# Every 512-column product names its columns from the last to the first: a two-block transformer on one core

## The chip, the core and the metric

The kernel runs on one core of a Trainium2 chip. The metric is device time in microseconds (us), the median of the timed runs. A core has a matrix engine (TensorE, PE in the profile; its weight loads are the row PEld), a vector engine (VectorE, DVE), a scalar engine (ScalarE, ACT), GpSimd (POOL) and a queue engine that issues transfers (SyncE, SP). They share the on-chip memory SBUF, and TensorE writes its sums to PSUM: 128 partitions with 8 banks of 512 32-bit numbers each.

## What is computed

The reference runs two blocks over 512 tokens of width 1024, all in 32-bit floats, cut here to what matters:

```
# first block
h = rmsnorm(x);  z = h @ w_in                        # latents, heads, two gates
qa = rmsnorm(q_lat) @ w_qb;  kva = rmsnorm(c_kv) @ w_kvb
oa = attention(qa, ka, va);  ob = attention(qb, kb, vb)      # 8 heads each
x += (sigmoid(gate_a) * (oa @ w_oa) + sigmoid(gate_b) * (ob @ w_ob)) @ w_o
x += (relu(rmsnorm(x) @ w_up) ** 2) @ w_down
x += sigmoid(rmsnorm(x) @ w_ple_gate) * (p @ w_ple)
x = rmsnorm(x)
# second block, layer 0: gated delta rule; layer 1: attention with a forget gate
for layer in 0, 1:
    x += rmsnorm(mixer[layer](rmsnorm(x)))           # w_in, w_out; w_kv, w_q, w_o
    x += rmsnorm(swiglu(rmsnorm(x)))                 # 1024 -> 2 * 2816 -> 1024
```

Nearly all arithmetic is in the products with weight matrices.

## The kernel before

**How a product is made.** Activations are held with features on the partitions and the 512 tokens along a partition, so a tile of 128 features is 128x512. To keep 32-bit accuracy each operand is split into a high part, rounded to the matrix engine's one-pass 32-bit type (`fp32r`), and a low part with what the rounding left. A product of a weight tile and an activation tile is then three matmuls into the same PSUM bank: high weight by high activation, high by low, low by high. The helper `product` (L437 to L443) issues these three. The helper `product_by_parts` (L446 to L458) does the same for the first weight chunk of a stage, but in the order in which the activation's parts become ready: the two matmuls on the high part (L452, L453) for two banks, then the one on the low part (L456) for both.

**What is stationary and what moves.** One operand of a matmul is loaded into the array, 128 columns of it (the weight load, PEld). The other, the moving tile, streams through in 512 columns; column j of it gives column j of the sum in the bank. In most stages the weights are stationary and the tokens move; where the result is wanted with tokens on the partitions (the gates and values of the second block, the last down product) the activations are stationary and 512 columns of the weights move. Both helpers are given the bank and the moving tile as 512 neighbouring elements per partition.

**What sets the order.** Weights come in chunks of 128x2048 that SP loads into two buffers in turn. ScalarE rounds a chunk to its high part (L223), VectorE subtracts to get the low part (L250), and TensorE waits for that and works the chunk off. The order on each engine is written out by hand, stage by stage; semaphores tie the engines together, and a bank is read by ScalarE or VectorE only once the last matmul of its sum has counted up `products`. Attention scores (L876), transposes, sums of squares and the small products of the delta rule call the matrix engine directly and not through the two helpers.

Of the kernel before, what the change touches and what calls it, by code (L numbers as in the profile page):

```python
# [4 lines left out]
P = 128  # L5
# [3 lines left out]
DT = D // P  # L9
# [382 lines left out]
def build_program(nc, w, plan, constants, tables, out):  # L392
# [11 lines left out]
    def place(name, at, shape, dtype=mybir.dt.float32):  # L404

        under = int(at * 256)
        if under == 0:
            with nc.sbuf_tensor(name, shape, dtype) as tensor:
                return tensor
        with nc.sbuf_tensor(name + "_under", [P, under], mybir.dt.float32), nc.sbuf_tensor(name, shape, dtype) as tensor:  # L410
            return tensor
# [5 lines left out]
    with ctx:  # L417
# [7 lines left out]
        psum = enter(nc.psum_tensor("psum", [P, 8, T], f32))  # L425
# [7 lines left out]
        def gain(name, tile=0):  # L433
            at = GAIN_AT[name] + tile
            return gains[:, at:at + 1]

        def product(bank, w_parts, a_parts, first, last):  # L437

            (wh, wl), (ah, al) = w_parts, a_parts  # L440
            nc.tensor.matmul(bank, wh, ah, start=first, stop=False)  # L441
            nc.tensor.matmul(bank, wh, al, start=False, stop=False)  # L442
            return nc.tensor.matmul(bank, wl, ah, start=False, stop=last)  # L443

        def product_by_parts(pe, k, banks, w_parts, x_parts, high_done, low_done):  # L446

            (wh, wl), (xh, xl) = w_parts, x_parts
            columns = [(bank, slice(m * P, (m + 1) * P)) for m, bank in enumerate(banks)]
            pe.wait_ge(high_done, k + 1)  # L450
            for bank, sl in columns:
                nc.tensor.matmul(psum[:, bank, :], wh[:, k, sl], xh, start=k == 0, stop=False)  # L452
                nc.tensor.matmul(psum[:, bank, :], wl[:, k, sl], xh, start=False, stop=False)  # L453
            pe.wait_ge(low_done, k + 1)
            for bank, sl in columns:
                last = nc.tensor.matmul(psum[:, bank, :], wh[:, k, sl], xl, start=False, stop=k == DT - 1)  # L456
                if k == DT - 1:
                    last.then_inc(weights.products, 1)  # L458

# [7 lines left out]
        def front(gates, split, q_a, k_a, v_a, qk_b, v_b):  # L467
# [25 lines left out]
            with stage("front", 152) as s:  # L493
# [23 lines left out]
                with nc.Block() as block:  # L517
# [15 lines left out]
                    def _(pe):  # L533
# [52 lines left out]
                        for k in range(DT):  # L586
                            product_by_parts(pe, k, (0, 1), (high, low), (split[:, 0, k, :], split[:, 1, k, :]),
                                             entry.high_done, entry.low_done)
# [7 lines left out]
                        for k in range(DT):  # L596
                            last = product(psum[:, 3, :], (high[:, k, at], low[:, k, at]),
                                           (split[:, 0, k, :], split[:, 1, k, :]), k == 0, k == DT - 1)
# [17 lines left out]
                        for n in range(Q_TILES):  # L616
                            bank = free(first_q + n)
                            for k in range(2):
                                last = product(psum[:, bank, :], [y[:, k, n * P:(n + 1) * P] for y in parts],
                                               (q_split[:, 0, k, :], q_split[:, 1, k, :]), k == 0, k == 1)  # L620
                            last.then_inc(weights.products, 1)
# [9 lines left out]
                        for j in range(TT):  # L631
                            if j >= 2:
                                pe.wait_ge(k_read, 2 * j - 2)
                            product(psum[:, 4 + j % 2, :], [y[:, 0, j * P:(j + 1) * P] for y in parts],
                                    latent, True, True).then_inc(weights.products, 1)
                            product(psum[:, free(first_v + j), :], [y[:, j * P:(j + 1) * P] for y in latent],
                                    [y[:, 0, HEADS * NOPE:] for y in parts], True, True).then_inc(weights.products, 1)
# [433 lines left out]
        class NextEntry:  # L1071
# [39 lines left out]
            def first_chunks(self, pe, start, banks):  # L1111

                lag = 1 if start + 1 in weights.apart else 4
                for i in range(DT + lag):
                    for c, k in ((0, i), (1, i - lag)):
                        if not 0 <= k < DT or 2 * c >= len(banks):
                            continue
                        if k == 0:
                            pe.wait_ge(weights.low_ready, start + c + 1)
                        high, low = weights.parts(Chunk(start + c), DT)  # L1120
                        if c == 0:
                            product_by_parts(pe, k, banks[0:2], (high, low), (self.split[:, 0, k, :], self.split[:, 1, k, :]),
                                             self.high_done, self.low_done)
                            continue
                        for m in range(2):
                            sl = slice(m * P, (m + 1) * P)
                            last = product(psum[:, banks[2 * c + m], :], (high[:, k, sl], low[:, k, sl]),
                                           (self.split[:, 0, k, :], self.split[:, 1, k, :]), k == 0, k == DT - 1)
                            if k == DT - 1:
                                last.then_inc(weights.products, 1)  # L1130
# [102 lines left out]
        class MixerOut:  # L1233
# [9 lines left out]
            def tensor(self, pe):  # L1243
                start, merged = self.start, self.merge.merged
                pe.wait_ge(self.merge.product_read, 12)
                pe.wait_ge(weights.low_ready, start + 1)
                high, low = weights.parts(Chunk(start), DT)
                for k in range(DT):
                    product_by_parts(pe, k, (0, 1), (high, low), (merged[:, 0, k, :], merged[:, 1, k, :]),
                                     self.merge.high_ready, self.merge.low_done)  # L1250
                for t in range(2, DT):
                    if t % 2 == 0:
                        pe.wait_ge(weights.low_ready, start + t // 2 + 1)
                    if t >= 4:
                        pe.wait_ge(self.added, t - 3)
                    whole_tile(start + t // 2, t % 2, t % 4, merged)
# [1974 lines left out]
        merged, part = place("merged", 64, [P, 2, DT, T], f32r), place("part", 96, [P, 2, 4, T])  # L3231
# [9 lines left out]
        columns, scratch = place("gdn_kept_columns", 120, [P, 8, TT * GH]), place("gdn_scratch", 121, [P, 6, T])  # L3241
# [86 lines left out]
        for name in ("ffn0", "fox_in", "ffn1"):  # L3328
            first = weights.start[name]
# [110 lines left out]
```

## Time and profile before

| | |
|---|---|
| median of 3 runs | 2165.18 us (2163.93 to 2165.28) |
| the profiled execution | 2162.32 us |
| its span, first to last instruction | 2160.5 us |
| TensorE busy | 2095.5 us (97%), 10710 matmuls |
| VectorE busy | 1146.3 us (53%) |
| ScalarE busy | 816.6 us (38%) |
| mean granted TensorE clock | 0.987 of full speed |

The profile is of one execution. Busy time is the union of an engine's instructions; the end of a matmul is modelled, and neighbouring matmuls overlap in it, so the pace of a stream of matmuls is read from their start times and not from their durations. An instruction's row names its operands' shape and type; the step between elements is not in it.

### The profile page before, as it was taken

How to read it: one execution, taken by the hardware profiler on the slowest of the kernel's cores; microseconds unless marked ns; L12 is line 12 of the kernel's file. 1: busy time of each engine (PE TensorE's matmuls, PEld its weight loads, DVE VectorE, ACT ScalarE, POOL GpSimd, SP SyncE). 2: the span in 40 equal slices, each digit the busy share in tenths (PEclk: the TensorE clock that was granted, in tenths of full speed). 3: DMA queues.
4: the chain of work that ended last, by engine and by line, in shares of the span. 5: the costliest groups of instructions: out<-in, count | busy, mean ns of one | idle time of the engine just before them, and what ended most of it. 6: DMA issues, size and time to landing. Idle time of an engine off the chain costs nothing. (4 is left out here: it accounts for less than half of the span.)

```text
span 2160.5 us, 26090 instructions
## 1 busy us (share of the span) xinstructions
PE 2095.5 (97%) x10710; PEld 1697.5 (79%) x10710; DVE 1146.3 (53%) x1706; ACT 816.6 (38%) x1169; POOL 38.4 (2%) x34
## 2 busy tenths in 40 slices
PE   8999999999999999999999999999999899999998
PEld 6876678888888887787878888887786577888886
DVE  5674765542542579888846444324634736444423
ACT  4324753331232465542534222213325734322212
POOL 0120000000000000000100000000000000000000
PEclk9999999999999999999999999999999999999999
DMA  4220012223223222233122222222240031222221
GB/s 177 86 83 35 2 59 99 94 95 109 85 96 103 91 81 100 108 117 97 40 98 74 95 95 94 95 96 95 98 173 23 1 118 59 98 98 98 98 98 68
DMA packets 43111, 190.68 MB, mean 88 GB/s; under 512 B 15520, under 2 KB 16224, under 8 KB 22384
## 3 DMA queue, kind: packets, MB, share of 16 engines
q1 hardware_dynamic: 40656, 184.78, 25.0%
q10 hardware_dynamic: 2336, 4.23, 0.6%
q8 instruction: 85, 1.39, 0.3%
q14 instruction: 34, 0.28, 0.0%
HBM read 185.25 MB, written 3.74 MB: 87 GB/s over the span
## 5 line engine op out<-in xcount | busy, mean ns | idle before, releaser
L250 DVE TENSOR_TENSOR weights_low<-weights_raw,weights_high 128x2048 fp32r<-128x2048 f32 (+1 forms) x161 | 365.8, 2272 | 565.4 <-ACT weights_high L223 565.3
L441 PE MATMUL psum<-split,weights_high 128*128 128x512 f32 x1448 | 568.3, 392 | 8.3 <-PEq L146 4.2
L442 PE MATMUL psum<-split,weights_high 128*128 128x512 f32 x1448 | 564.6, 390 | 0.0
L443 PE MATMUL psum<-split,weights_low 128*128 128x512 f32 x1448 | 564.6, 390 | 0.0
L223 ACT CAST weights_high<-weights_raw 128x2048 fp32r<-128x2048 f32 (+1 forms) x161 | 304.0, 1888 | 545.3 <-PE psum L443 504.7
L441 PEld LDWEIGHTS psum<-split,weights_high 128*128 128x128 f32 x1448 | 272.2, 188 | 70.3 <-issue 8.4
L443 PEld LDWEIGHTS psum<-split,weights_low 128*128 128x128 f32 x1448 | 272.0, 188 | 57.4
L442 PEld LDWEIGHTS psum<-split,weights_high 128*128 128x128 f32 x1448 | 272.0, 188 | 56.0
L443 PE MATMUL psum<-hidden_high,weights_low 128*128 128x512 f32 x256 | 99.6, 389 | 0.0
L441 PE MATMUL psum<-hidden_high,weights_high 128*128 128x512 f32 x256 | 99.6, 389 | 0.0
L442 PE MATMUL psum<-hidden_low,weights_high 128*128 128x512 f32 x256 | 99.6, 389 | 0.0
L2042 ACT ACTIVATE ring<-ring 128x512 f32<-128x512 f32 x44 | 27.8, 632 | 117.4 <-DVE ring L2072 117.4
L441 PE MATMUL psum<-hidden,weights_high 128*128 128x512 f32 x176 | 68.5, 389 | 0.0
L442 PE MATMUL psum<-hidden,weights_high 128*128 128x512 f32 x176 | 68.5, 389 | 0.0
L442 PE MATMUL psum<-weights_low,hidden 128*128 128x512 f32 x176 | 68.5, 389 | 0.0
L441 PE MATMUL psum<-weights_high,hidden 128*128 128x512 f32 x176 | 68.5, 389 | 0.0
L443 PE MATMUL psum<-hidden,weights_low 128*128 128x512 f32 x176 | 68.5, 389 | 0.0
L443 PE MATMUL psum<-weights_high,hidden 128*128 128x512 f32 x176 | 68.5, 389 | 0.0
L452 PE MATMUL psum<-split,weights_high 128*128 128x512 f32 x112 | 48.0, 428 | 17.3 <-DVE weights_low L250 10.2
L2530 DVE SCALAR_TENSOR_TENSOR gdn_spare<-psum,conv,gdn_spare 128x511 f32<-128x511 f32 (+2 forms) x72 | 53.8, 747 | 11.0 <-ACT gdn_spare L2363 9.3
L938 DVE TENSOR_REDUCE attn_small<-psum 128x1 f32<-128x512 f32 x64 | 42.5, 688 | 30.6 <-PE psum L876 30.6
L442 PEld LDWEIGHTS psum<-hidden_low,weights_high 128*128 128x128 f32 x256 | 48.0, 188 | 10.1
(485 smaller groups left out, 3081.4 us busy)
## 6 DMA issues: line engine op xcount, KB each, us to landing
weights_raw<-in_weights SPq DMA_DIRECT2D x161, 1024.0 KB, 4.9
minus_c<-minus_c_rows ACTq DMA_DIRECT2D x16, 256.0 KB, 7.3
x_stream<-in_x SPq DMA_DIRECT2D x4, 512.0 KB, 7.1
gdn_in_grown<-gdn_rows SPq DMA_DIRECT2D x4, 512.0 KB, 4.7
chain_grown<-gdn_rows SPq DMA_DIRECT2D x4, 512.0 KB, 3.7
out<-end_results SPq DMA_DIRECT2D x8, 256.0 KB, 2.1
table<-rope_tables SPq DMA_DIRECT2D x1, 1024.0 KB, 12.0
weights_raw<-in_weights SPq DMA_DIRECT2D x1, 768.0 KB, 4.2
```

The source lines that it names most:

```text
L223: self.nc.scalar.copy(self.high_of(chunk.first)[:, 0:width], self.raw[:, chunk.slot, 0:width]).then_inc(self.high_ready, 1)
L250: self.nc.vector.tensor_tensor(out=self.low_of(n)[:, 0:width], in0=self.raw[:, n % 2, 0:width], in1=self.high_of(n)[:, 0:width].bitcast(se ...
L441: nc.tensor.matmul(bank, wh, ah, start=first, stop=False)
L442: nc.tensor.matmul(bank, wh, al, start=False, stop=False)
L443: return nc.tensor.matmul(bank, wl, ah, start=False, stop=last)
L452: nc.tensor.matmul(psum[:, bank, :], wh[:, k, sl], xh, start=k == 0, stop=False)
L938: nc.vector.tensor_reduce(small[:, 0, u:u + 1], psum[:, u % 4, 0:n], AX.X, ALU.max, negate=True).then_inc(max_ready, 1)
L2042: nc.scalar.activation(self.tanh[:, f % 2, :], self.gate[:, f % 2, :], ACT.Tanh, scale=0.5).then_inc(self.tanh_ready, 1)
L2530: nc.vector.scalar_tensor_tensor(out=mixed[:, o % 2, back:T], in0=psum[:, bank_of(o), 0:T - back], scalar=conv[:, at:at + 1], in1=mixed[:, ...
```

## The change

A small helper gives a view of a tile with its columns in descending order (a step of -1, beginning at the last element). Both product helpers take this view of the moving tile and of the PSUM bank. Column j of the moving tile still gives column j of the bank; only the order in which the columns are named in the instruction is turned round. The stationary tile, the matmuls that don't go through the two helpers, and everything on the other engines stay as they were. The instructions of each of the five engines, with their waits, are the same in number and order as before.

```
+        def from_the_end(tile):
+            return tile[:, ::-1]
+
         def product(bank, w_parts, a_parts, first, last):
-            (wh, wl), (ah, al) = w_parts, a_parts
-            nc.tensor.matmul(bank, wh, ah, start=first, stop=False)
-            nc.tensor.matmul(bank, wh, al, start=False, stop=False)
-            return nc.tensor.matmul(bank, wl, ah, start=False, stop=last)
+            (wh, wl), (ah, al) = w_parts, (from_the_end(part) for part in a_parts)
+            out = from_the_end(bank)
+            nc.tensor.matmul(out, wh, ah, start=first, stop=False)
+            nc.tensor.matmul(out, wh, al, start=False, stop=False)
+            return nc.tensor.matmul(out, wl, ah, start=False, stop=last)

         def product_by_parts(pe, k, banks, w_parts, x_parts, high_done, low_done):
-            (wh, wl), (xh, xl) = w_parts, x_parts
-            columns = [(bank, slice(m * P, (m + 1) * P)) for m, bank in enumerate(banks)]
+            (wh, wl), (xh, xl) = w_parts, (from_the_end(part) for part in x_parts)
+            columns = [(from_the_end(psum[:, bank, :]), slice(m * P, (m + 1) * P)) for m, bank in enumerate(banks)]
             pe.wait_ge(high_done, k + 1)
             for bank, sl in columns:
-                nc.tensor.matmul(psum[:, bank, :], wh[:, k, sl], xh, start=k == 0, stop=False)
-                nc.tensor.matmul(psum[:, bank, :], wl[:, k, sl], xh, start=False, stop=False)
+                nc.tensor.matmul(bank, wh[:, k, sl], xh, start=k == 0, stop=False)
+                nc.tensor.matmul(bank, wl[:, k, sl], xh, start=False, stop=False)
             pe.wait_ge(low_done, k + 1)
             for bank, sl in columns:
-                last = nc.tensor.matmul(psum[:, bank, :], wh[:, k, sl], xl, start=False, stop=k == DT - 1)
+                last = nc.tensor.matmul(bank, wh[:, k, sl], xl, start=False, stop=k == DT - 1)
```

## Rows read from the trace of the kernel before

**Rows 1.** The page: busy time (share of span) and instructions; granted clock by slice.

```profile
PE 2095.5 (97%) x10710; PEld 1697.5 (79%) x10710; DVE 1146.3 (53%) x1706; ACT 816.6 (38%) x1169; POOL 38.4 (2%) x34
...
PEclk9999999999999999999999999999999999999999
```

**Rows 2.** Who waited for whom, TensorE: us in total, times, longest.

```profile
PE psum L452 <- DVE weights_low L250: 10.2, 1, 10.2
PE psum L889 <- DVE ring L959: 8.1, 8, 1.7
PE psum L452 <- ACT split L1087: 7.1, 3, 2.4
```

**Rows 3.** Busy time and count, whole span, of L441, L442, L443, L452, L453, L456.

```profile
0.00:2161.00 2161.00, 960.69 (x2452) 460.19 (x2452) 0.99 0.26 88
...
0.00:2161.00 2161.00, 955.95 (x2452) 460.20 (x2452) 0.99 0.26 88
...
0.00:2161.00 2161.00, 955.96 (x2452) 460.14 (x2452) 0.99 0.26 88
...
0.00:2161.00 2161.00, 60.52 (x144) 29.03 (x144) 0.99 0.26 88
...
0.00:2161.00 2161.00, 59.41 (x144) 29.21 (x144) 0.99 0.26 88
...
0.00:2161.00 2161.00, 47.09 (x144) 28.22 (x144) 0.99 0.26 88
```

**Rows 4.** Timeline of TensorE in the first block's down product: start us, us, instruction.

```profile
500.09 0.39 PE L441 MATMUL psum<-hidden_high,weights_high 128*128 128x512 f32 x1
500.31 0.39 PE L442 MATMUL psum<-hidden_low,weights_high 128*128 128x512 f32 x1
500.54 0.39 PE L443 MATMUL psum<-hidden_high,weights_low 128*128 128x512 f32 x1
...
501.45 0.39 PE L441 MATMUL psum<-hidden_high,weights_high 128*128 128x512 f32 x1
```

**Rows 5.** Stretches: from:to, us, each engine's busy us (x instructions), then granted clock.

```profile
500.00:580.00 80.00, 80.00 (x355) 66.24 (x354) 29.38 (x28) 17.29 (x12) 0.00 (x0) 1.00 0.27 92
...
1498.20:1508.40 10.20, 7.13 (x18) 5.22 (x19) 8.61 (x15) 5.75 (x10) 0.00 (x0) 0.50 0.00 1
```

**Rows 6.** Timeline of TensorE at the start of the forget block's products.

```profile
1505.21 0.63 PE L452 MATMUL psum<-split,weights_high 128*128 128x512 f32 x1
1505.64 0.63 PE L453 MATMUL psum<-split,weights_low 128*128 128x512 f32 x1
1506.07 0.63 PE L452 MATMUL psum<-split,weights_high 128*128 128x512 f32 x1
1506.49 0.63 PE L453 MATMUL psum<-split,weights_low 128*128 128x512 f32 x1
1506.92 1.05 PE L456 MATMUL psum<-split,weights_high 128*128 128x512 f32 x2
```

**Rows 7.** Attention scores: a stretch, then line L876's durations (ns) and timeline.

```profile
188.00:242.00 54.00, 53.01 (x359) 33.40 (x360) 35.00 (x75) 35.76 (x90) 0.00 (x0) 1.00 0.00 1
...
L876 PE MATMUL psum<-k_a,q_a x64: 591/592/697, 189.0 to 242.1; 96*128 96x512 f32 x64
...
195.09 1.88 PE L876 MATMUL psum<-k_a,q_a 96*128 96x512 f32 x4
```

**Rows 8.** Timeline of ScalarE and VectorE, 500 to 510 us, with idle time before.

```profile
499.66 1.91 ACT L223 CAST weights_high<-weights_raw 128x2048 fp32r<-128x2048 f32 x1 [8.97 <-PE psum L443]
...
501.60 2.29 DVE L250 TENSOR_TENSOR weights_low<-weights_raw,weights_high 128x2048 fp32r<-128x2048 f32 x1 [8.59 <-ACT weights_high L223]
```

**Rows 9.** Timeline of the end: TensorE's last matmul and VectorE's last work.

```profile
2150.94 0.39 PE L443 MATMUL psum<-weights_high,hidden 128*128 128x512 f32 x1
...
2156.12 1.20 DVE L1882 TENSOR_TENSOR end_results<-end_results,turned_x 128x512 f32<-128x512 f32 x1
```

## The prediction, made before the changed kernel had run

> **What bounds the kernel now.** I read the page's table of busy time first. TensorE is busy 2095.5 us of a span of 2160.5 us, VectorE about half of it, ScalarE a third, and the granted clock stands at nine tenths or more in every slice [rows 1]. Then the table of waits, for TensorE alone: the longest entry is one wait of 10.2 us at the very start, and the next come to 8.1 and 7.1 us [rows 2]. So TensorE is the bound nearly everywhere, and what happens to its pace goes into the time one for one.
>
> Next, how much of that pace the change touches. The six lines of the two product helpers, counted over the whole span, give 2452 matmuls on each of three lines and 144 on each of the other three [rows 3]: 3 x 2452 + 3 x 144 = 7788 matmuls, all with 512 moving columns. Their durations cannot be added up, since 390 ns records overlap. The pace is in the start times: from 500.09 to 501.45 us six starts pass [rows 4], 1.36 us / 6 = 0.227 us each. The stretch from 500 to 580 us says the same over a longer run: 80 us fully busy with 354 weight loads, one for each matmul, 80 / 354 = 0.226 us at a granted clock of 1.00 [rows 5]. I take 0.2265 us. 7788 x 0.2265 = 1764 us, or 82% of the span, is spent in matmuls that the change rewrites.
>
> What that pace is made of matters below. At the full clock (the upper level, 2.4 GHz) 512 columns at one per cycle take 512 / 2.4 = 213.3 ns, so 13.2 ns of each product are something fixed. In a stretch where the granted clock was 0.50 (the lower level, 1.2 GHz) [rows 5], with TensorE at work for only 7.13 of 10.20 us, the same products start at 1505.21, 1505.64, 1506.07, 1506.49 and 1506.92 us [rows 6]: 1.71 / 4 = 0.4275 us, which is 512 / 1.2 = 426.7 ns and next to nothing fixed.
>
> **The change, part by part.** It removes no instruction, adds none and moves none. Each engine has the same instructions in the same order with the same waits, so there is no queue in which something new stands, no transfer that starts at another moment for its own sake, and no wait that takes the place of another. Every one of the 7788 matmuls has the same number of columns. The stationary tile, and with it the weight load, is named as before. What is left is one question asked 7788 times: does TensorE take 512 columns in descending order as fast as in ascending order, when it reads them from SBUF and when it adds them into the bank?
>
> No row of the trace answers it. The records hold no step, and in the program before, every moving tile of the 7788 runs upwards. So I bound the price of one product from both sides.
>
> Below: the stream itself cannot go faster than one column per cycle at the upper clock level, which is 213.3 ns. If the descending order did away with the whole fixed part, a product would gain 13.2 ns: 7788 x 13.2 ns = 103 us.
>
> Above: the nearest rows in which 512 columns take longer on this engine both give about 0.43 us. One is the half clock just read. The other is at a granted clock of 1.00: the scores of the first attention, products of the ordinary 32-bit type, in which four matmuls of 512 columns take 1.88 us with a last one of 592 ns [rows 7], (1.88 - 0.592) / 3 = 0.429 us from start to start, half the pace of the one-pass type at the same clock. If descending columns were served one by one where ascending ones are served in pairs, this is the pace that I expect. The difference is 0.429 - 0.2265 = 0.2025 us per product, times 7788 = 1577 us. A few tens of the products run at the half clock already, which takes some 10 us off.
>
> Which value I take: zero. The nearest row is the product itself, with the same number of elements in the same places: 512 neighbours in SBUF, 512 neighbours in one bank. The sum is 2162.3 us (the profiled execution: its span of 2160.5 us and 1.8 us around it) + 7788 x 0 = 2162.3 us. The median of the runs shown is 2165.2 us, 2.9 us or 0.13% above this execution, and as nothing is added to either I name the median: 2165.2 us.
>
> Here a rule speaks against the change. The Trainium skill, "PSUM — Partial Sum Buffer", section "Specifications (TRN2)", gives PSUM lines of 8 bytes and says that any non-contiguous access pattern slows matmuls significantly; it names no price. By it, if a step of -1 counts as non-contiguous, the sum would be somewhere above 2165 us. "Advanced Engine Details and Errata" of the Trainium skill, section "Memory Cachelines", words it so that every two consecutive elements should be contiguous for best throughput; by that wording columns 511 and 510, which share a line, are as good as 0 and 1, and the sum stays. No run here has shown a stepped product, so the trace does not yet decide between the two.
>
> **What lies beside it.** If the products stay at their pace, nothing else can move, because everything else is cued by them. ScalarE's rounding of a chunk takes 1.91 us after 8.97 us of idling for TensorE, and VectorE's subtraction 2.29 us after 8.59 us of idling for ScalarE [rows 8]. With that much idle time they stay off the path, and all the more if TensorE becomes slower. After the last matmul, which starts at 2150.94 us, VectorE works until 2156.12 + 1.20 = 2157.3 us [rows 9], 3.2 us before the span ends; this tail reads complete banks and does not care in which order their columns were filled.
>
> **The rivals.**
>
> First, pairs that are lost. TensorE at the upper clock level reads or adds two neighbours in one access only if the second lies above the first; descending, each column needs an access of its own. For it: the ordinary 32-bit type shows that this engine does run at 0.429 us per 512 columns when it has to [rows 7], and with 97% busy nothing would hide it. Against it: that pace belongs to another type, and no row ties it to addresses. It decides for the whole kernel as soon as one side, reading or adding, has the limit. Price: 2162 + 1577 - 10 = about 3730 us. The first of the two wordings of the Trainium skill above, on "PSUM — Partial Sum Buffer", points the same way.
>
> Second, a start-up cost per product. Each matmul begins at the far end of its tile and of its bank, and if the first fetch then covers less than it does now, some nanoseconds are added that the stream cannot make good. For it: the fixed 13.2 ns at the full clock [rows 4, 5] show that there is something at the seam between two products. Against it: at the half clock nothing is left of it [rows 6], and the 512 elements begin and end on the same borders in both directions. Price: from 1 ns (7.8 us, 2173 us) to as much again as now, 13.2 ns, 2165 + 103 = 2268 us. It becomes measurable from 0.56 ns per product.
>
> Third, the other sign: the fixed part shrinks, for instance if the seam is a matter of the last columns of one sum being added while the first of the next arrive. Against it: both directions jump from one end of the bank to the other between two products. Price: 2165 - 103 = 2062 us if all of it goes.
>
> That the change does not do what it says, because the order is turned back on the way to the chip, would give 2165 us as well and belongs to the main case.
>
> **How the numbers follow.** A measurement of this kernel can tell about 0.2%, 4.3 us, from no change; per product that is 0.56 ns. Chances: no change 0.77, lost pairs 0.08, a start-up cost 0.10, a gain 0.05. So faster by over 0.2% has 0.05, within 0.2% 0.77, slower by over 0.2% 0.18. The predicted time is that of the likeliest case, 2165.2 us. The range reaches into the neighbouring cases: down to 2150 us, a gain of 2 ns per product (7788 x 2 ns = 16 us), and up to 2205 us, a cost of 5 ns per product (39 us). With 0.77 inside, about 0.06 of the start-up case and 0.02 of the gain, it holds about 0.85. Left out are lost pairs, whose 3730 us would make a range of which nine tenths is empty, and the far ends of the other two.
>
> **What would show it right or wrong.** Right: in the down product around 500 us the starts are still 0.226 to 0.227 us apart, the stretch of 80 us still holds about 354 weight loads, and TensorE's busy time is within a few us of 2095.5. Lost pairs: starts 0.43 us apart at a granted clock of 1.00, while the attention scores keep their own pace, and longer waits of ScalarE's rounding for TensorE. Start-up cost: starts a few nanoseconds further apart, evenly in all stages, and no other row changed. A gain: starts nearer to 0.213 us. I am wrong in kind if the starts in [rows 4] are the same after the change and the time is not; then something other than the stream reads the order of the columns.

## The result: 2% slower, and the profile after

The changed kernel takes 2207.27 us (2206.16 to 2209.87), the kernel before 2165.14 us beside it: a ratio of 1.0198, 95% interval 1.018 to 1.0215. No change had been forecast, with a range up to 2205 us. The profiled execution's span is 2205.1 us, against 2160.5 us.

TensorE is as much the bound as before. The page's row of busy time after, which answers to [rows 1], shows 46.7 us more on PE and next to nothing on the others:

```profile
PE 2142.2 (97%) x10710; PEld 1698.2 (77%) x10710; DVE 1146.6 (52%) x1706; ACT 814.9 (37%) x1169; POOL 38.5 (2%) x34
```

The counts of the product lines (now L445, L446, L447 and L456, L457, L460) are those of [rows 3]. The first and the fourth of these rows after, in the same columns:

```profile
0.00:2206.00 2206.00, 979.30 (x2452) 460.40 (x2452) 0.99 0.25 86
...
0.00:2206.00 2206.00, 60.76 (x144) 28.77 (x144) 0.99 0.25 86
```

So the time went into the pace of the same matmuls. The timeline of TensorE after, in the same down product as [rows 4] (start us, us, instruction):

```profile
500.20 0.40 PE L446 MATMUL psum<-hidden_low,weights_high 128*128 128x512 f32 x1
500.43 0.40 PE L447 MATMUL psum<-hidden_high,weights_low 128*128 128x512 f32 x1
500.67 0.40 PE L445 MATMUL psum<-hidden_high,weights_high 128*128 128x512 f32 x1
...
501.60 0.40 PE L446 MATMUL psum<-hidden_low,weights_high 128*128 128x512 f32 x1
```

Six starts in 1.40 us are 0.2333 us each, where six took 1.36 us before. The stretches, columns as in [rows 5], say it for 80 us at a granted clock of 1.00, and give a stretch at the half clock:

```profile
500.00:580.00 80.00, 80.00 (x345) 64.46 (x343) 24.85 (x21) 14.74 (x8) 0.00 (x0) 1.00 0.27 92
1531.90:1538.80 6.90, 5.99 (x14) 4.47 (x15) 6.87 (x12) 4.97 (x8) 0.00 (x0) 0.51 0.00 0
```

343 weight loads stand where 354 stood. At the half clock nothing has changed; the timeline there answers to [rows 6]:

```profile
1535.64 0.63 PE L456 MATMUL psum<-split,weights_high 128*128 128x512 f32 x1
1536.07 0.63 PE L457 MATMUL psum<-split,weights_low 128*128 128x512 f32 x1
1536.50 0.63 PE L456 MATMUL psum<-split,weights_high 128*128 128x512 f32 x1
1536.92 0.63 PE L457 MATMUL psum<-split,weights_low 128*128 128x512 f32 x1
1537.35 1.05 PE L460 MATMUL psum<-split,weights_high 128*128 128x512 f32 x2
```

(1537.35 - 1535.64) / 4 = 0.4275 us, as before. The attention scores, which keep their order, have the median duration of [rows 7], 592 ns:

```profile
L880 PE MATMUL psum<-k_a,q_a x64: 591/592/1061, 192.7 to 247.5; 96*128 96x512 f32 x64
```

The other engines only wait longer: VectorE's 137 waits for a rounded chunk come to 589.2 us, 565.3 before. And the sum closes to within 3 us. Over all pairs of neighbouring product starts at the full clock that are less than 260 ns apart, the mean is 226.91 ns before and 233.35 ns after: 6.44 ns x 7788 = 50.2 us. The span grew by only 44.6 us, because this execution spent less time at the half clock: with mean granted clocks of 0.987 and 0.991 the clock cost 0.013 x 2160.5 = 28 us before and 0.009 x 2205.1 = 20 us after, which leaves 42 us of the 50.2.

### The profile page after: what moved, and what is told of

Read it like the earlier page. It is cut to its first block and busy times, and to the rows that moved or that the text cites. A ratio compares the mean times of both kernels' runs of the same rounds, so it can differ in the third digit from the quotient of the medians.

```text
span 2205.1 us, 26090 instructions
## 1 busy us (share of the span) xinstructions
PE 2142.2 (97%) x10710; PEld 1698.2 (77%) x10710; DVE 1146.6 (52%) x1706; ACT 814.9 (37%) x1169; POOL 38.5 (2%) x34
## 5 line engine op out<-in xcount | busy, mean ns | idle before, releaser
L250 DVE TENSOR_TENSOR weights_low<-weights_raw,weights_high 128x2048 fp32r<-128x2048 f32 (+1 forms) x161 | 365.4, 2270 | 589.3 <-ACT weights_high L223 589.2
L445 PE MATMUL psum<-split,weights_high 128*128 128x512 f32 x1448 | 578.7, 400 | 8.0 <-PEq L146 4.5
L446 PE MATMUL psum<-split,weights_high 128*128 128x512 f32 x1448 | 575.5, 397 | 0.0
L447 PE MATMUL psum<-split,weights_low 128*128 128x512 f32 x1448 | 575.4, 397 | 0.0
L445 PEld LDWEIGHTS psum<-split,weights_high 128*128 128x128 f32 x1448 | 272.0, 188 | 77.0 <-issue 7.2
L447 PEld LDWEIGHTS psum<-split,weights_low 128*128 128x128 f32 x1448 | 271.9, 188 | 66.0
L446 PEld LDWEIGHTS psum<-split,weights_high 128*128 128x128 f32 x1448 | 272.0, 188 | 64.0
L445 PE MATMUL psum<-hidden_high,weights_high 128*128 128x512 f32 x256 | 101.7, 397 | 0.0
L446 PE MATMUL psum<-hidden_low,weights_high 128*128 128x512 f32 x256 | 101.7, 397 | 0.0
L447 PE MATMUL psum<-hidden_high,weights_low 128*128 128x512 f32 x256 | 101.7, 397 | 0.0
L445 PE MATMUL psum<-hidden,weights_high 128*128 128x512 f32 x176 | 69.9, 397 | 0.0
L447 PE MATMUL psum<-hidden,weights_low 128*128 128x512 f32 x176 | 69.9, 397 | 0.0
L445 PE MATMUL psum<-weights_high,hidden 128*128 128x512 f32 x176 | 69.9, 397 | 0.0
L446 PE MATMUL psum<-hidden,weights_high 128*128 128x512 f32 x176 | 69.9, 397 | 0.0
L446 PE MATMUL psum<-weights_low,hidden 128*128 128x512 f32 x176 | 69.9, 397 | 0.0
L447 PE MATMUL psum<-weights_high,hidden 128*128 128x512 f32 x176 | 69.9, 397 | 0.0
L456 PE MATMUL psum<-split,weights_high 128*128 128x512 f32 x112 | 48.0, 428 | 17.0 <-DVE weights_low L250 9.9
L447 PEld LDWEIGHTS psum<-hidden_high,weights_low 128*128 128x128 f32 x256 | 48.1, 188 | 11.7
```

The source lines that it names most:

```text
L250: self.nc.vector.tensor_tensor(out=self.low_of(n)[:, 0:width], in0=self.raw[:, n % 2, 0:width], in1=self.high_of(n)[:, 0:width].bitcast(se ...
L445: nc.tensor.matmul(out, wh, ah, start=first, stop=False)
L446: nc.tensor.matmul(out, wh, al, start=False, stop=False)
L447: return nc.tensor.matmul(out, wl, ah, start=False, stop=last)
L456: nc.tensor.matmul(bank, wh[:, k, sl], xh, start=k == 0, stop=False)
```

## The experiments

The mean start distances below are taken as just described, between neighbouring matmuls of the same kind. "Up" is from the first column to the last, "down" the reverse.

**Reading or adding.** e1 turns only the moving tile round, e2 only the bank (shortened; `product_by_parts` likewise):

```
# e1: product                        # e2: product
-            out = from_the_end(bank) -  (ah, al) = ..., (from_the_end(part) for part in a_parts)
+            out = bank               +  (ah, al) = ..., a_parts
```

> Only the moving tile is named from the last column to the first; the bank is named upwards as before (the sums land with their columns turned round, so the output is not the reference's). In the changed kernel the products start 233.4 ns apart at the full clock, before 226.7 ns. Theory A (the reading of the moving tile costs the 6.7 ns): starts 233 to 234 ns apart, time about 2207 us, ratio to before 1.02. Rival B (the adding into the bank costs it): starts 226 to 227 ns apart, about 2165 us, ratio 1.00. Rival C (each side costs a part): starts near 230 ns, about 2186 us. In all of them 427 ns at the half clock.

> Only the bank is named from the last column to the first; the moving tile is named upwards as before (the sums land with their columns turned round, so the output is not the reference's). Theory A (the reading costs): starts 226 to 227 ns apart, about 2165 us, ratio 1.00. Rival B (the adding costs): starts 233 to 234 ns apart, about 2207 us, ratio 1.02. Rival C (each a part): near 230 ns, about 2186 us.

e1 took 2206.94 us, ratio 1.0203 (1.0185 to 1.0222); e2 2163.16 us, ratio 1.0003 (0.9991 to 1.0014). Timeline of e1:

```profile
519.81 0.40 PE L445 MATMUL psum<-hidden_high,weights_high 128*128 128x512 f32 x1
520.05 0.40 PE L446 MATMUL psum<-hidden_low,weights_high 128*128 128x512 f32 x1
520.28 0.40 PE L447 MATMUL psum<-hidden_high,weights_low 128*128 128x512 f32 x1
520.51 0.40 PE L445 MATMUL psum<-hidden_high,weights_high 128*128 128x512 f32 x1
```

and of e2:

```profile
519.87 0.39 PE L445 MATMUL psum<-hidden_high,weights_high 128*128 128x512 f32 x1
520.10 0.39 PE L446 MATMUL psum<-hidden_low,weights_high 128*128 128x512 f32 x1
520.32 0.39 PE L447 MATMUL psum<-hidden_high,weights_low 128*128 128x512 f32 x1
520.55 0.39 PE L445 MATMUL psum<-hidden_high,weights_high 128*128 128x512 f32 x1
```

Three starts take 0.70 us in e1 and 0.68 us in e2. The whole cost comes with the order in which the moving tile is read; adding into the bank downwards costs nothing that these runs can tell (their interval ends at 1.0014).

**Per matmul or per column.** e3 splits each matmul into two of 256 columns, e4 does so with each half downwards (shortened):

```
+            for n, half in enumerate((slice(0, 256), slice(256, 512))):
+                done = nc.tensor.matmul(from_the_end(bank[:, half]), w, from_the_end(a[:, half]), ...)   # e4
```

> Every product matmul of 512 columns is made as two of 256 columns, both upwards; the base line for the next run. If the fixed 13.3 ns at the full clock belong to each matmul: 106.7 + 13.3 = 120 ns from start to start, about 240 ns for a pair and about 2165 + 7788 x 0.0133 = 2269 us. If they belong to each 512 columns: about 113 ns, 2165 us, unless the weight load of each holds it up.

> The same two matmuls of 256 columns, each with its moving tile and its part of the bank named from the last column to the first. Theory S (a start-up cost of each matmul): starts 6.7 ns further apart than with the halves upwards, so the time is about 15576 x 6.7 ns = 104 us above that run. Rival D (a cost that grows with the columns, 6.7 ns for 512): 3.3 ns further apart, about 52 us above it.

One run each: 2257.68 us up and 2234.14 us down; neighbours under 140 ns apart start 120.0 and 118.3 ns apart on the mean. For e3 that is its first case, a fixed part that belongs to each matmul. Of e4's two theories both failed, in sign. The stretch from 500 to 580 us of e3, then of e4:

```profile
500.00:580.00 80.00, 80.00 (x669) 80.00 (x668) 16.45 (x8) 14.49 (x8) 0.00 (x0) 1.00 0.27 93
```

```profile
500.00:580.00 80.00, 80.00 (x678) 80.00 (x678) 18.28 (x12) 13.40 (x7) 0.00 (x0) 1.00 0.29 95
```

More matmuls pass downwards than upwards in the same time, so at 256 columns a downward matmul has no dearer start than an upward one. The pair has a limit: there are twice as many weight loads, and they are busy for all of the 80 us (66.24 us in [rows 5]), so that the loads may set part of this pace was not tested.

**Lengths and turns.** e5 varies the middle matmul of each product, e7 turns every second one (shortened):

```
+  down(bank, wh, ah); nc.tensor.matmul(bank[:, 0:448][:, ::-1], w, a[:, 0:448][:, ::-1], ...); down(bank, wl, ah)   # e5, one of 17
+  step = -1 if turns[0] % 2 else 1;  nc.tensor.matmul(bank[:, ::step], w, a[:, ::step], ...)                       # e7
```

> The middle matmul of each product (high weights by low activations) is given other lengths and directions, 20 products at a time, each on its own line; the other two go over 512 columns, all down where the middle one is down, all up where it is up, and mixed in two of the cases. Columns that the middle matmul leaves out are missing from the sums. From 226.7 ns (512 up), 120.05 ns (256 up), 233.35 ns (512 down) and 118.4 ns (256 down) two lines follow. Theory D2 (going down the columns themselves are slower, 0.449 ns each against 0.417, and the fixed part is smaller, 3.5 ns against 13.4): down 448, 384, 320, 256 columns take 204.6, 175.9, 147.2, 118.4 ns; up 200.0, 173.4, 146.7, 120.0 ns; the two cross near 300 columns. Rival S2 (the same 0.417 ns per column both ways, and a seam between two matmuls that depends on where the one stops and the next begins): going down from a place to column 0, N/2.4 + 20 ns whatever N is: 206.7, 180.0, 153.3, 126.7 ns; and a matmul up among ones down, or down among ones up, has yet another seam, so those two cases differ from 226.7 and 233.35 ns. By D2 alone a down matmul among ones up keeps its 0.449 ns per column, 229.9 ns plus a fixed part.

> Every second product matmul is named downwards, the others upwards, moving tile and bank alike. Theory D2 (slower columns going down, a fixed part that belongs to each direction): starts by turns 226.7 and 233.35 ns apart, mean 230, time about 2165 + 3894 x 6.65 ns = 2191 us, ratio 1.012. Rival S2 (the seam is set by where the one stops and the next begins): an up matmul stops at column 511 where the next, down, begins, and that one stops at column 0 where the next begins; with no jump at the seam the fixed part shrinks: as low as 216 to 220 ns, 2165 - 7788 x 8 ns = about 2100 us, ratio 0.97; or, if a place just read is the worst to begin at, above 233 ns.

In e5 20 products of each kind follow one another. The starts of the first middle matmul of the blocks with 512, 448, 384, 320 and 256 columns, all down:

```profile
614.62 0.40 PE L447 MATMUL psum<-split,weights_high 128*128 128x512 f32 x1
628.63 0.37 PE L449 MATMUL psum<-hidden_low,weights_high 128*128 128x448 f32 x1
642.09 0.34 PE L451 MATMUL psum<-hidden_low,weights_high 128*128 128x384 f32 x1
655.03 0.31 PE L453 MATMUL psum<-hidden_low,weights_high 128*128 128x320 f32 x1
667.29 0.28 PE L455 MATMUL psum<-hidden_low,weights_high 128*128 128x256 f32 x1
```

A product of three takes 14.01 / 20 = 700.5 ns with 512 columns in the middle, then 673, 647 and 613 ns. By D2 it would have been 233.35 x 2 + 204.6 = 671, 643 and 614; by a cost independent of length, 700 less 26.7, 53.3 and 80 = 673, 647 and 620. Neither line fits all three. Upwards, with upward neighbours, the same lengths take 680, 663, 638, 620 and 587 ns (medians). Going down is thus 20 ns dearer with 512 columns in the middle, 10 and 9 ns with 448 and 384, 7 ns cheaper with 320, and level with 256. The two outer matmuls alone would account for 2 x 6.4 = 13 ns, so a shortened middle matmul shows no extra cost of its own.

The mixed cases do not add up by one rule either. One matmul down between two up takes 687.0 ns, the sum by D2. One up between two down takes 700.2 ns, as much as three down, where D2 gives 693.6. And 504 upward columns, of tile and bank, that begin 32 bytes further on take 693.4 ns in place of 680.6 with all 512, so place plays a part as well as direction. Many of the distances come near to multiples of 6.67 ns, 16 cycles of the full clock: 226.7 is 34, 233.3 is 35, 700 is 105, 673.3 is 101, 646.7 is 97, 613.3 is 92. The 118.3 ns of the downward halves, a mean of distances from 115 to 123 ns, is none. e7 took 2189.51 us, ratio 1.0108 (1.0085 to 1.0132), near D2's 2191; its distances alternate between about 233 and 227 ns, so doing away with the jump between two matmuls brings nothing.

**The order itself.** e6 and e10 take the columns in blocks:

```
+        def view(t, c, outer, inner):
+            return t.rearrange("p (b c) -> p b c", c=c)[:, ::outer, ::inner]
```

> All three matmuls of a product take the 512 columns in one of eleven orders, 24 products at a time, each order on its own line; moving tile and bank alike, so the sums are the reference's. Blocks of 256, 64, 16, 4 or 2 columns are taken from the last to the first with ascending columns inside, or from the first to the last with descending columns inside. Up 226.7 and down 233.35 ns are the controls. Theory D2 (neighbours going down are slower to read): blocks with descending columns inside cost about what down costs, 233 ns, however small the block down to 4; blocks from the last to the first with ascending columns inside cost 226.7 ns for 256 and 64, and more only for the smallest. Rival S2 (only the place where a matmul stops and the next begins counts): inner order plays no part; orders that begin at the end of the tile cost 233, those that begin near its start 227 ns. By both, half pace (427 ns) would show for blocks of 2 or 4 if reading needed an access per block.

> As the run with eleven orders, for blocks of 128, 32 and 8 columns (512, 128 and 32 bytes), 24 products at a time: blocks from the last to the first with ascending columns inside, or from the first to the last with descending columns inside. Theory U (what counts is the order of the 16-byte pieces inside each aligned 256 bytes of the moving tile; the order of these units, and the order inside 16 bytes, do not count): blocks of 128 backwards 226.9 ns as up, blocks of 32 and 8 backwards 233.3 ns as down; descending inside 128 columns 233.3 ns, inside 32 more than 233.3 and up to 267 ns, inside 8 between 226.9 and 267 ns. Rival G (each jump to a lower address costs, so fewer jumps are cheaper): blocks of 128, 32 and 8 backwards rise in that order from 227 ns by the number of their jumps, 3, 15 and 63, and blocks of 8 backwards cost far more than 233.3 ns.

A line's durations (ns, min/median/max) show the pace: in the controls of e6, L447 up and L449 down, 389 goes with 226.95 ns from start to start and 397 with 233.4. Then from last to first 64-column (L455) and 16-column blocks (L459), 16-column blocks descending inside (L461), and 4-column blocks descending inside (L465):

```profile
L447 PE MATMUL psum<-split,weights_high x168: 387/389/486, 23.7 to 1979.9; 128*128 128x512 f32 x168
L449 PE MATMUL psum<-split,weights_high x216: 396/397/480, 42.3 to 1996.7; 128*128 128x512 f32 x108
L455 PE MATMUL psum<-split,weights_high x304: 389/389/504, 101.0 to 2046.2; 128*128 128x512 f32 x152
L459 PE MATMUL psum<-split,weights_high x408: 397/397/503, 140.3 to 2076.9; 128*128 128x512 f32 x136
L461 PE MATMUL psum<-split,weights_high x248: 427/432/511, 158.4 to 1911.7; 128*128 128x512 f32 x124
L465 PE MATMUL psum<-split,weights_high x192: 387/389/476, 311.7 to 1945.9; 128*128 128x512 f32 x192
```

The mean start distances of both runs, in ns:

| columns in a block | blocks backwards, inside up | blocks forwards, inside down |
|---|---|---|
| 256 | 227.0 | 233.4 |
| 128 | 227.0 | 233.4 |
| 64 | 227.2 | 233.5 |
| 32 | 232.4 | 234.5 |
| 16 | 233.4 | 266.7 |
| 8 | 233.5 | 233.2 |
| 4 | 233.3 | 226.9 |
| 2 | 233.4 | not run |

With the tiles where the kernel before has them, what matters is the order of 16-byte pieces within 256 bytes. Units of 64 columns (256 bytes) and more may be taken in any order; inside four columns (16 bytes) the order is free too. In between, leaving the ascending order costs about one step of 6.67 ns (233.4 against 226.9 ns), and the worst order six (266.7 ns). The bank was named in the same block order as the moving tile; that the bank's order is free is shown for a step of -1 alone (e2). D2 missed the 4-column blocks, S2 the inner order. Of e10's two theories, U (256-byte units) fits all six entries but one detail: descending inside 32 columns costs hardly more than 233.3. Rival G (jumps) falls, as 63 backward jumps (8 columns) cost no more than 31 (16 columns). The Trainium skill ("SBUF — State Buffer", section "Door 1: The DMA port swizzle") says that consecutive accesses to the same 16-byte line hit full bandwidth; the free order inside four columns agrees, at 226.9 ns.

**Is it the weight load?** During a product the next weights are read too: the loads are busy for 66.24 of 80 us in [rows 5]. e8 keeps that reading in one place or cuts it to 32 columns; three kernels move all activation tiles by 64, 128 and 512 bytes:

```
+        def same(t):                                                       # e8: stationary tile
+            return t[:, 0:1].broadcast_to([P, t.shape[1]])
-        enter(nc.sbuf_tensor("arena_offset", [P, 40], f32))                # offsets: 56, 72, 168; later 104
+        enter(nc.sbuf_tensor("arena_offset", [P, 56], f32))
```

> The stationary tile is varied, 24 products at a time, each form on its own line: as it is, or its first column named 128 times over (a step of 0, so the weight load stays at one place), or, in the middle matmul alone, 32 columns of it instead of 128; the moving tile goes up, down, or up in blocks of 16 columns with descending columns inside (the sums then lack most of the weights, or a quarter of the rows of one term, and the output is not the reference's). Theory W (the extra time of a product is the moving tile's reading held up by the weight load's reading, which goes on during it, in steps of 6.7 ns: 2 steps up, 3 down, 8 in blocks of 16): with the load at one place the extra time changes with the weights although the moving tile is read as before: near 213 to 220 ns up and down alike, and the blocks of 16 fall from 267 ns to near 220; with 32 columns the middle matmul costs at most one or two steps, in each direction. Rival M (the reading of the moving tile alone): 226.7, 233.3 and 266.7 ns whatever the weights are.

> The kernel before, with everything upwards, but all tiles from the activations on lie 64 bytes further on in each partition; the weights stay where they were. Theory W: the steps in which the two readings hold each other up depend on how the two addresses stand to each other, so the starts move from 226.7 ns to another multiple of 6.7 ns (213 to 267 ns), one way or the other, in all stages. Rival M: the moving tile's own place on a 64-byte border is kept, 226.7 ns and 2165 us.

> The same with 128 bytes. Theory W: starts 213 to 267 ns apart in steps of 6.7 ns, different from 226.7 if the distance of the two addresses counts below 256 bytes. Rival M: 226.7 ns, 2165 us.

> The same with 512 bytes, the length of a weight load in a partition. Theory W: different from 226.7 ns if the distance counts at this size, else as before. Rival M: 226.7 ns, 2165 us.

e8, with its weights at one place, down (L456) and in blocks of 16 (L460); the median durations stay near the 397 and 432 ns above:

```profile
L456 PE MATMUL psum<-split,weights_high x376: 393/397/501, 93.7 to 2067.1; 128*128 128x512 f32 x188
L460 PE MATMUL psum<-split,weights_high x304: 431/437/530, 123.9 to 2105.5; 128*128 128x512 f32 x152
```

Their mean start distances are 233.3 and 266.7 ns whatever the weights, and 32 weight columns in the middle matmul gave 233.4 ns down. Theory W falls for these. Up, weights at one place gave 231.5 instead of 227.0 ns, and 32 weight columns 233.0 ns after the middle matmul: the weights count, but with a rise that neither theory had. In the offset runs rival M failed as well: upwards the mean distance is 229.5 ns at 64 bytes (2179.82 us) and 232.4 ns at 128 (2204.32 us), and 226.9 ns again at 512 (2162.51 us). So for the upward order place counts, and that led to the last two runs.

> The kernel before, all upwards, with all tiles from the activations on 256 bytes further on. 64 and 128 bytes made the mean start distance 229.5 and 232.4 ns, 512 bytes left it at 226.9. Theory U (units of 256 bytes): 226.9 ns and about 2164 us. Rival V (units of 512 bytes or more): between 229 and 240 ns, 2175 to 2260 us.

> The changed kernel, all downwards, with the tiles 64 bytes further on. Theory U (a downward tile gains nothing from the border): 233.3 ns as without the offset, about 2207 us. Rival V (the border counts for both directions): another 2 to 6 ns, 2220 to 2250 us.

The stretch from 500 to 580 us: upwards with 64, 128 and 256 bytes of offset, one kernel each, then downwards with 64:

```profile
500.00:580.00 80.00, 80.00 (x351) 65.68 (x351) 27.69 (x25) 14.58 (x9) 0.00 (x0) 1.00 0.28 98
```

```profile
500.00:580.00 80.00, 80.00 (x346) 64.88 (x345) 23.34 (x19) 13.95 (x8) 0.00 (x0) 1.00 0.27 93
```

```profile
500.00:580.00 80.00, 80.00 (x355) 66.24 (x354) 29.27 (x28) 17.39 (x12) 0.00 (x0) 1.00 0.27 92
```

```profile
500.00:580.00 80.00, 80.00 (x345) 64.45 (x344) 24.71 (x21) 14.87 (x8) 0.00 (x0) 1.00 0.27 92
```

256 bytes: 226.9 ns and 2160.07 us, as before. Down with 64 bytes: 233.3 ns and 2209.41 us, as the changed kernel. Both are the numbers of theory U: the upward pace comes back with 256 bytes, and the downward order loses nothing by 64 bytes.

But the reason that U gives, the upward tile's own border, does not hold, and the offset traces show it. In the last down product of the second block the weights move and the activations are stationary, so an offset leaves the moving tile in its place and shifts only the stationary one. There too the pace falls. Before, then with 64 bytes:

```profile
2040.00:2140.00 100.00, 100.00 (x443) 82.81 (x442) 20.75 (x10) 18.67 (x11) 0.00 (x0) 1.00 0.23 80
```

```profile
2060.00:2160.00 100.00, 100.00 (x431) 80.21 (x429) 19.69 (x9) 16.45 (x12) 0.00 (x0) 1.00 0.23 79
```

100 us / 442 = 226.2 ns and 100 / 429 = 233.1 ns. Two weight tiles, `early_high` and `early_low`, lie among the activations and are shifted with them. The kernel with 128 bytes uses them beside weights that were not shifted, with the same moving tiles (`split`):

```profile
1169.99 0.39 PE L441 MATMUL psum<-split,early_high 128*128 128x512 f32 x1
...
1171.12 0.40 PE L443 MATMUL psum<-split,early_low 128*128 128x512 f32 x1
1171.36 0.40 PE L452 MATMUL psum<-split,weights_high 128*128 128x512 f32 x1
1171.60 0.40 PE L453 MATMUL psum<-split,weights_low 128*128 128x512 f32 x1
1171.83 0.39 PE L452 MATMUL psum<-split,weights_high 128*128 128x512 f32 x1
1172.06 0.39 PE L453 MATMUL psum<-split,weights_low 128*128 128x512 f32 x1
...
1175.52 0.39 PE L441 MATMUL psum<-split,early_high 128*128 128x512 f32 x1
...
1178.02 0.39 PE L443 MATMUL psum<-split,early_low 128*128 128x512 f32 x1
```

With shifted weights five distances take 1.13 us and eleven take 2.50 us, 0.226 and 0.227 us each; with weights in their old place three take 0.70 us, 0.233 us each. The means over the whole execution, in ns, before and with 64 and 128 bytes (pairs of the same kind, under 260 ns):

| shifted | pairs | before | 64 bytes | 128 bytes |
|---|---|---|---|---|
| the moving tile alone | 6540 to 6557 | 226.9 | 229.0 | 232.5 |
| the stationary tile alone | 910 | 226.8 | 233.3 | 232.4 |
| both | 120 or 121 | 226.9 | 227.3 | 227.6 |

So the upward order is quick when the moving and the stationary tile lie alike within 256 bytes, at the offsets that were run. That is what theory W said of the two addresses, and for the upward order it stands; for the downward order it does not, as 64 bytes leave 233.3 ns whichever of the two is shifted. None of the forms run here is quicker than the kernel before.

## Why the prediction was wrong

**What bounds the kernel: right.** TensorE's pace went into the time one for one, on exactly the 7788 matmuls counted, and no other engine took anything back.

**The step that failed: "Which value I take: zero."** Its argument was that the descending order visits the same aligned groups, each once and whole, "and only the order of the groups and the order within one is turned", and that a cost "would need hardware that knows neighbours only in one direction". That holds for the adding side (e2, ratio 1.0003). For the reading side (e1, ratio 1.0203) it holds inside 16 bytes and for whole units of 256 bytes, but not in between: e6 and e10 find the cost there, 6.4 ns per product, and 6.44 x 7788 = 50 us is the term that I had set at 0. The argument also took the weight load as untouched because it is "named as before". The offset runs show that the pace of the upward order depends on where the stationary tile lies, so reading the moving tile could not be weighed by itself.

**The bounds held, the range did not.** A product's price lay between -13.2 and +202.5 ns as worked out, and the measured 6.4 ns lies inside. The upper end of the range, 2205 us, stood for 5 ns per product: I had cut the second rival in the middle of its own span of 1 to 13.2 ns without a row to cut by.

**The rivals.** Lost pairs did not come. The second had the form right, "starts a few nanoseconds further apart, evenly in all stages, and no other row changed", and the hint that nothing is left of it at the half clock (0.4275 us before and after). Its price, 1 to 13.2 ns, held the 6.4 ns, but not for its reason: halves down pass more quickly than halves up (118.3 against 120.0 ns), a shortened middle matmul shows no extra cost, and 64-column blocks from the last to the first, ascending inside, begin in the tile's last block and take 227.2 ns. So it isn't a start-up cost of each matmul. The third, a gain, appeared only in those halves, which are slower as a whole, and with 320 columns in the middle in e5 (613 against 620 ns).

**The rule that spoke against the change.** The Trainium skill's words in "PSUM — Partial Sum Buffer", section "Specifications (TRN2)", that any non-contiguous pattern slows matmuls, are not borne out for a step of -1 in the bank: e2 shows 226.9 ns. The gentler wording in "Advanced Engine Details and Errata", section "Memory Cachelines", two neighbours together, agrees with it, though that section repeats the harsher sentence too. I had weighed the sum's side with a rule and passed over the side that is read, where the cost was.

**What stays open.** Why the steps are of 6.7 ns, why a weight load that stays at one place makes the upward order 4.5 ns slower, and what holds up the reading at all. The runs show that the cost comes with the order of the moving tile, and that the upward pace depends on how that tile lies to the stationary one. That the two readings get in each other's way fits this, but it is not shown: why the downward order takes 233.3 ns whatever the weights and their place stays open.

## What to carry to other kernels

When a stream of one-pass 32-bit matmuls is the bound, keep the moving tile ascending, and let it and the stationary tile lie alike within 256 bytes of a partition: here the order cost 2% of the time, and 128 bytes between the two 2.4% of each product (232.4 against 226.9 ns). Where a change alters only how operands are named, a "same elements, same cost" argument is a guess until one side at a time has been run; the reading and the adding side behave differently. A cost of nanoseconds is worth a wide upper end in the range when thousands of instructions on the bound carry it.

## What was not expected of the hardware

- Upward order is not quick because it is upward: blocks of 64 columns taken from the last to the first pass at 227.2 ns, an upward tile 128 bytes off its place at 232.5 ns, and at 227.6 ns when the stationary tile is shifted with it.
- Blocks of 16 columns forwards with descending columns inside take 266.7 ns per product, 40 ns more than up, and blocks of 4 such columns 226.9 ns.
- Two downward matmuls of 256 columns take 236.7 ns, two upward ones 239.9 ns.
- At the half clock, products up and down both start 0.4275 us apart: the penalty exists at the full clock only.
